# Gated stage: half centred beside its squares, root put into copies of the mixing weights, first mixing three steps later

## The chip, the cores and the metric

One core of a Trainium2 chip runs the whole program in one launch. The metric is the device time of that core in microseconds, the median of several executions. Data lie in float32 with the 128 partitions as rows of a tile of positions; a matrix product is made of three TensorE passes on a high and a low part.

## The reference

Sixteen stages over 256 positions of 1024 numbers, for two models one after the other: feed-forward stages, one mixer of each kind per layer, and an embedding stage. The change is in the second stage, the gated mixer (N = 2048 numbers per half, 8 groups of 256, blocks of 128 positions):

```python
z = jax.nn.gelu(h @ w_in + b_in)
u, v = jnp.split(z, 2, axis=-1)
mean = jnp.mean(vf, axis=-1, keepdims=True)
var = jnp.mean(jnp.square(vf - mean), axis=-1, keepdims=True)
v = (vf - mean) * lax.rsqrt(var + LN_EPS) * v_gain
ws = jnp.where(mask[None], w_s, 0)
s = jnp.einsum('gij,bcjgd->bcigd', ws, v) + b_s.T[None, None, :, :, None]
y = (u * s).reshape(B, S, GMLP_WIDTH)
return y @ w_out
```

The mean and the variance belong to a position j, and j is the index over which the mixing product sums. So the root of position j may stand with v (a row of it) or with column j of ws.

## The kernel before

The program is written out by hand for each engine; the order on an engine is the order of the code, and semaphores join the engines. There are two tiles t of 128 positions. `made`, `moved`, `product` and the like are counters: one semaphore each, raised by one engine in its program order, so that a wait for an entry is a wait for all before it.

Each matrix layer (`linear`, L505 to L507) goes through its weights in parts of two 128-row slices by 512 columns. The input layer of the gated stage has 8 blocks of 512 output columns, 4 parts each (part i, 32 in all), in the order v, v, v, v, u, u, u, u. A step is the three matmuls of one slice and one tile, so a part is 4 steps and block b has steps 16b + 1 to 16b + 16; part i has steps 4i + 1 to 4i + 4. `during(step)` puts other TensorE work ahead of a step.

For each part ScalarE makes the rounded copy `wh` (L623, "cast" below) and VectorE the remainder `wl` (L809, "remainder i"). There are seven buffers of each, so both work up to seven parts ahead: in the loop over parts, turn i handles part i + 7. Raw weights come from SyncE's queue in chunks of two parts, into three buffers; a chunk is asked for when the remainders of the chunk three before it are made.

The gated stage's own work:

- After block b, VectorE puts scale and bias on the two tiles' result (L1259, "bias work of block b"), and ScalarE's gelu writes v into `TMP` (blocks 0 to 3, L1209, with a sum) or u into `gU` (blocks 4 to 7, L1214).
- After block 3, `dve_layer_norm` (L1285 on): VectorE takes the mean (L1291, L1294), ScalarE sums the squares of v less the mean in four pieces, tile t and half a of 1024 columns, order (0,0), (0,1), (1,0), (1,1) (L1223). VectorE adds the halves (L1296), POOL makes the root (L1001, L1003), and VectorE centres and scales (L1303) and multiplies by v_gain (L1307), piece by piece, half 0 of both tiles first.
- v_gain and the bias rows are copied by DMA from POOL's queue to all partitions (`spread`, L996) into three buffers `bc`; a copy waits until its buffer's last reader is done. The second half of v_gain takes the buffer of the bias of blocks 2 and 3.
- `pe_gmlp_mix(c)` (L1173) multiplies two groups of v by the masked, turned mixing weights `gW`, for both tiles, into banks 6 and 7. The mixings c = 0, 1, 2 stand ahead of steps 82, 98 and 114, and c = 3 ahead of step 127.
- `dve_gmlp_gated(c)` (L1277) adds b_s and multiplies by u. `pe_gmlp_turn` (L1183) transposes the result in two turnings per mixing (ahead of steps 90 and 91 for c = 0), using banks 6 and 7 in turn, ScalarE copies it to `gYH` (L1233), VectorE makes its remainder `gYL` (L1283). Only then is the bank free for the next mixing.

On VectorE, turn i of the loop is: gating if i is 20, 24 or 28; turned remainder if i is 22, 26 or 30; the remainder of part i + 7; bias work if i is 3, 7, 11 and so on. In the text, "remainder 23" is that of part 23, made in turn 16.

## Time and profile before

| | |
|---|---|
| three timed runs | 2326.01, 2326.09, 2327.51 us; median 2326.09 |
| the profiled execution's own time | 2319.1 us |
| its span | 2317.3 us |
| mean granted TensorE clock | 0.988 |
| TensorE busy | 2245.4 us, 97% |
| VectorE, ScalarE, POOL busy | 63%, 50%, 8% |
| chain that ended last | TensorE 81%, VectorE 4%, ScalarE 2% |
| DMA | 395.60 MB, mean 171 GB/s |

The span is from the first to the last instruction of one execution taken by the profiler, and its own time is 1.8 us longer; the timed runs are others. Times inside the trace are microseconds from the span's start. In a timeline an entry is one instruction, or several of one kind that follow each other (x2, x4), and the bracket gives the idle time before it and what ended it. PE is TensorE, DVE is VectorE, ACT is ScalarE.

### The profile page before, as it was taken

To read this page: it belongs to the slowest core of one execution; us is meant where nothing else is said; L and a number is where in the kernel's file an instruction comes from. 1 tells how busy PE (TensorE), PEld (TensorE's weight loads), DVE (VectorE), ACT (ScalarE), POOL (GpSimd) and SP (SyncE) were. 2 spreads that over 40 slices of the span, in tenths; PEclk is the share of its full clock that TensorE was granted. 3 is DMA by queue.
4 is the path that set the end of the run, shared out by engine and by line. 5 is a ranking of instruction groups with operands and counts; after the bars stand their busy time and mean duration, and the time that the engine had idled before them with its cause. 6 is when DMAs were issued, how large, how long until landed. Compare 5 with 4: busy or idle time off the path is not lost.

```text
span 2317.3 us, 33592 instructions
## 1 busy us (share of the span) xinstructions
PE 2245.4 (97%) x13285; PEld 1822.6 (79%) x13285; DVE 1467.5 (63%) x2077; ACT 1156.8 (50%) x1670; POOL 181.4 (8%) x289
## 2 busy tenths in 40 slices
PE   8999999999999899989999999999999999979998
PEld 6888788888888658768887888877888888758887
DVE  6656657656765877576567656656656765647655
ACT  5445545445544464254455445455445544545444
POOL 1001001001000011320011001001001000051001
PEclk9999999999999999999999999999999999989999
DMA  7556556554655540065556555525554655506553
GB/s 250 185 194 205 180 181 195 182 189 165 211 188 191 198 140 11 4 196 190 182 183 199 185 195 197 175 82 177 182 183 172 209 183 198 176 20 201 189 177 109
DMA packets 290074, 395.60 MB, mean 171 GB/s; under 512 B 11736, under 2 KB 193312, under 8 KB 289920
## 3 DMA queue, kind: packets, MB, share of 16 engines
q1 hardware_dynamic: 285072, 377.20, 49.0%
q0 software_dynamic: 4704, 16.20, 2.0%
q8 instruction: 107, 1.75, 0.3%
q14 instruction: 47, 0.39, 0.1%
q10 hardware_dynamic: 144, 0.07, 0.0%
HBM read 392.37 MB, written 1.05 MB: 170 GB/s over the span
## 4 chain that ended last, share of the span: by engine, by line
PE 81%; DVE 4%; ACT 2%; issue 1%; POOL 1%; DVEq 0%; POOLq 0%; ACTq 0%
PE bank L505 24%; PE bank L507 24%; PE bank L506 24%; PE bank L531 1%; PE bank L519 1%; DVE qPS L1863 0%; PE bank L2507 0%; PE bank L2501 0%; PE bank L1435 0%; DVE wl L809 0%; ACT JUNK L630 0%; ACT qPS L1808 0%; PE bank L2518 0%; PE bank L1921 0%; POOL rSM L1003 0%
## 5 line engine op out<-in xcount | busy, mean ns | idle before, releaser
L809 DVE TENSOR_TENSOR wl<-raw,wh 128x1024 fp32r<-128x1024 f32 x708 | 858.8, 1223 | 566.5 <-ACT wh L623 566.2
L623 ACT ACTIVATE wh<-raw 128x1024 fp32r<-128x1024 f32 x708 | 744.3, 1058 | 654.8 <-PE bank L507 633.5
L505 PE MATMUL bank<-wh,XH 128*128 128x512 f32 x2000 | 804.5, 402 | 19.4 <-DVE XL L2132 4.7
L506 PE MATMUL bank<-wl,XH 128*128 128x512 f32 x2000 | 783.8, 392 | 0.0
L507 PE MATMUL bank<-wh,XL 128*128 128x512 f32 x2000 | 783.7, 392 | 0.0
L505 PEld LDWEIGHTS bank<-wh,XH 128*128 128x128 f32 x2000 | 378.4, 189 | 109.8 <-issue 24.9
L507 PEld LDWEIGHTS bank<-wh,XL 128*128 128x128 f32 x2000 | 377.9, 189 | 82.1
L506 PEld LDWEIGHTS bank<-wl,XH 128*128 128x128 f32 x2000 | 378.8, 189 | 73.1 <-issue 0.5
L505 PE MATMUL bank<-wh,AH 128*128 128x512 f32 x704 | 276.0, 392 | 0.0
L507 PE MATMUL bank<-wh,AL 128*128 128x512 f32 x704 | 274.1, 389 | 0.0
L506 PE MATMUL bank<-wl,AH 128*128 128x512 f32 x704 | 274.1, 389 | 0.0
L507 PEld LDWEIGHTS bank<-wh,AL 128*128 128x128 f32 x704 | 132.1, 188 | 27.8
L506 PEld LDWEIGHTS bank<-wl,AH 128*128 128x128 f32 x704 | 132.2, 188 | 26.7
L505 PEld LDWEIGHTS bank<-wh,AH 128*128 128x128 f32 x704 | 132.2, 188 | 26.6
L1024 POOL TENSOR_SCALAR ST<-ST 128x1 f32<-128x1 f32 x32 | 8.6, 268 | 1363.2 <-ACT JUNK L630 1363.0
L723 ACT ACTIVATE AH<-bank 128x512 fp32r<-128x512 f32 x88 | 52.8, 600 | 114.6 <-PE bank L531 114.6
L927 DVE TENSOR_TENSOR AL<-bank,AH 128x512 fp32r<-128x512 f32 x88 | 60.8, 691 | 58.1 <-ACT AH L723 58.1
L957 DVE SCALAR_TENSOR_TENSOR att<-att,ST,bank 128x256 f32<-128x256 f32 x176 | 84.6, 481 | 6.2
L753 ACT ACTIVATE att<-bank,ST 128x256 f32<-128x256 f32 x176 | 72.5, 462 | 12.7 <-POOL ST L1064 12.7
L954 DVE SCALAR_TENSOR_TENSOR att<-att,bank 128x256 f32<-128x256 f32 x176 | 72.9, 414 | 5.2 <-ACT att L753 5.2
L635 ACT ACTIVATE XH<-CT 128x512 fp32r<-128x512 f32 x60 | 37.2, 628 | 77.4 <-DVE CT L826 72.7
L630 ACT ACTIVATE JUNK<-bank 128x512 bf16<-128x512 f32 x48 | 28.4, 591 | 55.2 <-PE bank L507 55.0
(332 smaller groups left out, 1720.1 us busy)
## 6 DMA issues: line engine op xcount, KB each, us to landing
raw<-in_ffn_w_dram SPq DMA_DIRECT2D x182, 512.0 KB, 4.6
raw<-in_ffn_wi_dram SPq DMA_DIRECT2D x176, 512.0 KB, 4.6
raw<-in_ffn_w_dram SPq DMA_DIRECT2D x40, 1024.0 KB, 4.9
raw<-in_ffn_wo_dram SPq DMA_DIRECT2D x40, 1024.0 KB, 4.9
raw<-in_a_wqkv_dram SPq DMA_DIRECT2D x18, 1024.0 KB, 4.8
raw<-in_a_w_in_dram SPq DMA_DIRECT2D x16, 1024.0 KB, 5.6
raw<-in_b_w_in_dram SPq DMA_DIRECT2D x12, 1024.0 KB, 4.9
bc<-in_norm_g_dram POOLq DMA_DIRECT2D x16, 512.0 KB, 5.2
```

What stands on the lines that cost most here:

```text
L505: pe.e.matmul(o, a, h, start=(k == 0), stop=False)
L506: pe.e.matmul(o, a, l, start=False, stop=False)
L507: m = pe.e.matmul(o, b, h, start=False, stop=(k == layer.nk - 1))
L623: act.e.activation(self.wh[j % N_W][:, 0:p.size], self.raw[p.chunk % N_RAW][:, p.at:p.at + p.size], ACT.Copy).then_inc(*self.rounded.up(j))
L630: act.e.activation(self.JUNK[:, 0:x.shape[-1]], x, ACT.Square, accum_out=total).then_inc(*self.squared.up(*key))
L635: act.e.activation(self.XH[:, 4 * b:4 * b + 4, t * P:(t + 1) * P], self.CT[b][:, :, :], ACT.Copy).then_inc(*self.x_hi.up(n, t, b))
L723: act.e.activation(self.AH[:, 2 * b:2 * b + 2, :], bank.rearrange("p (k s) -> p k s", k=2), ACT.Copy).then_inc(*self.hid_hi.up(n, b))
L753: act.e.activation(self.att[b % 3][:, t * FB:(t + 1) * FB], self.pair((n, "up", b))[t][:, 0:FB], ACT.Tanh, scale=sc[:, t:t + 1]).then_inc( ...
L809: dve.e.tensor_tensor(self.wl[j % N_W][:, 0:p.size], self.raw[p.chunk % N_RAW][:, p.at:p.at + p.size], self.wh[j % N_W][:, 0:p.size].bitca ...
L927: dve.e.tensor_tensor(lo, bank.rearrange("p (k s) -> p k s", k=2), hi.bitcast(F32), ALU.subtract).then_inc(*self.hid_lo.up(n, b))
L954: dve.e.scalar_tensor_tensor(x, x, 1.0, pair[:, 0:FB], ALU.add, ALU.mult).then_inc(*self.gate.up(n, b, t))
L957: dve.e.scalar_tensor_tensor(x, x, sc[:, T + t:T + t + 1], pair[:, FB:2 * FB], ALU.mult, ALU.mult).then_inc(*self.gated.up(n, b, t))
```

## The change

It does five things in the gated stage.

1. VectorE's eight passes over v become four, (v + (-mean)) * v_gain in one instruction each, tile 0 first; each waits for the square sum of its own piece alone, as ScalarE reads v before it is overwritten. The addition of the variance's halves stands ahead of the last of them.
2. The root is multiplied into the mixing weights: `gW` becomes tile 0's (in place) and a new buffer `gWR[1]` tile 1's, two VectorE instructions of 128 x 1024. Position j is the partition of the turned weights, so the root is one number per partition. `gWR[1]` lies in the last quarter of `gYL`'s place.
3. The DMA of v_gain's second half is issued ahead of POOL's root instead of behind it.
4. On TensorE the first mixing goes from ahead of step 82 to ahead of step 85, its turnings from 90 and 91 to 92 and 93.
5. On VectorE the bias work of block 4 goes from turn 19 to turn 17, and the first gating from turn 20 to turn 19.

```diff
--- before.py
+++ after.py
@@ -316,6 +316,9 @@
         self.gYL = at("gYL", EO + 16384, [P, 16, S], F32R)
 
 
+        self.gWR = [self.gW, at("gWR", EO + 28672, [P, 8, P], F32)]
+
+
         wide = [P, T, D]
         self.R = at("rR", EO, wide, F32)
         self.K = at("rK", EO + 8192, wide, F32)
@@ -1145,10 +1148,11 @@
                                            self.ident[:, :])
                     m.then_inc(*self.turned.up("ws", q))
             for c in range(3):
-                if step == 16 * (5 + c) + 2:
+                if step == 16 * (5 + c) + (5, 2, 2)[c]:
                     self.pe_gmlp_mix(pe, c)
-                if step in (16 * (5 + c) + 10, 16 * (5 + c) + 11):
-                    self.pe_gmlp_turn(pe, 2 * c + step % 16 - 10)
+                turn = 16 * (5 + c) + (12, 10, 10)[c]
+                if step in (turn, turn + 1):
+                    self.pe_gmlp_turn(pe, 2 * c + step - turn)
             if step == 16 * 7 + 15:
                 self.pe_gmlp_mix(pe, 3)
 
@@ -1166,11 +1170,11 @@
         self.place["pair", ("mix", g2)] = 3
         for t in range(T):
             bank = self.take_bank(pe, 6 + t, (self.made, "y", g2, t))
-            pe.wait_ge(self.made, "ws")
             pe.wait_ge(self.made, "v", g2 // 2, t)
+            pe.wait_ge(self.made, "wr", t)
             for h in range(2):
                 g = 2 * g2 + h
-                m = pe.e.matmul(bank[:, h * 256:(h + 1) * 256], self.gW[:, g, :],
+                m = pe.e.matmul(bank[:, h * 256:(h + 1) * 256], self.gWR[t][:, g, :],
                                 self.TMP[:, t, g // 4, (g % 4) * 256:(g % 4) * 256 + 256], start=True, stop=True)
             m.then_inc(*self.product.up("mix", g2, t))
 
@@ -1242,13 +1246,13 @@
             if i == 5:
                 dve.wait_ge(self.moved, "ws", 1)
                 dve.e.memset(self.gW[64:128, :, 0:64], 0.0).then_inc(*self.made.up("ws"))
-            if i >= 20 and i % 4 == 0:
-                self.dve_gmlp_gated(dve, i // 4 - 5)
+            if i == 19 or i > 20 and i % 4 == 0:
+                self.dve_gmlp_gated(dve, (i + 1) // 4 - 5)
             if i >= 20 and i % 4 == 2:
                 self.dve_gmlp_turned(dve, i // 4 - 5)
             self.leave(dve, p.j + N_W)
-            if i % 4 == 3:
-                b = i // 4
+            if i == 17 or i != 19 and i % 4 == 3:
+                b = 4 if i == 17 else i // 4
                 bias = self.place["bc", ("bias", b // 2)]
                 for t in range(T):
                     dve.wait_ge(self.used[t], layer.end[b])
@@ -1292,19 +1296,22 @@
             *self.made.up("mean"))
         dve.wait_ge(self.made, "mean")
         dve.e.tensor_scalar(nmean, mean, -1.0 / 2048, None, ALU.mult).then_inc(*self.made.up("nmean"))
-        dve.wait_ge(self.squared, "var", 1, 1)
-        dve.e.tensor_tensor(r, var[:, 0:T], var[:, T:2 * T], ALU.add).then_inc(*self.made.up("var"))
+        dve.wait_ge(self.made, "nmean")
+        for t in range(T):
+            for a in range(2):
+                g = self.place["bc", ("v_gain", a)]
+                x = self.TMP[:, t, a, :]
+                dve.wait_ge(self.squared, "var", t, a)
+                if (t, a) == (1, 1):
+                    dve.e.tensor_tensor(r, var[:, 0:T], var[:, T:2 * T], ALU.add).then_inc(*self.made.up("var"))
+                dve.wait_ge(self.d_bc[g], "v_gain", a)
+                dve.e.scalar_tensor_tensor(x, x, nmean[:, t:t + 1], self.bct[g][:, :], ALU.add, ALU.mult).then_inc(
+                    *self.made.up("v", a, t))
         dve.wait_ge(self.rs, "ln")
-        dve.wait_ge(self.made, "nmean")
-        for a in range(2):
-            g = self.place["bc", ("v_gain", a)]
-            for t in range(T):
-                x = self.TMP[:, t, a, :]
-                dve.e.tensor_scalar(x, x, nmean[:, t:t + 1], r[:, t:t + 1], ALU.add, ALU.mult).then_inc(
-                    *self.made.up("centred", a, t))
-                dve.wait_ge(self.d_bc[g], "v_gain", a)
-                dve.wait_ge(self.made, "centred", a, t)
-                dve.e.tensor_tensor(x, x, self.bct[g][:, :], ALU.mult).then_inc(*self.made.up("v", a, t))
+        dve.wait_ge(self.made, "ws")
+        for t in (1, 0):
+            m = dve.e.tensor_scalar(self.gWR[t][:, :, :], self.gW[:, :, :], r[:, t:t + 1], None, ALU.mult)
+            m.then_inc(*self.made.up("wr", t))
 
     def pool_gmlp(self, pool, n):
         A = self.A
@@ -1319,12 +1326,10 @@
                 self.pool_rs(pool, n)
             if q == 3:
                 for a in range(2):
-                    if a == 1:
-                        r = self.cols(T, "lnr")
-                        pool.wait_ge(self.made, "var")
-                        self.rsqrt(pool, r, 1.0 / 2048, LN_EPS, "ln")
                     i = self.spread(pool, A["a_v_gain"][0, a * 1024:(a + 1) * 1024], "v_gain", a)
                     self.bc_busy[i] = [(self.made, "v", a, 1)]
+                pool.wait_ge(self.made, "var")
+                self.rsqrt(pool, self.cols(T, "lnr"), 1.0 / 2048, LN_EPS, "ln")
             c = order[q]
             i = self.spread(pool, bias[c * 512:c * 512 + 1024], "bias", q)
             self.bc_busy[i] = [busy[q]]
```

VectorE, the place from the mean of block 3's end to the last pass (ST holds the small columns, bc_76 and bc_77 the halves of v_gain). Before:

```order
L1291 TENSOR_REDUCE ST<-ST 128x2
L1294 TENSOR_SCALAR ST<-ST 128x2
L1296 TENSOR_TENSOR ST<-ST 128x2
L1303 TENSOR_SCALAR TMP<-TMP,ST 128x1024
L1307 TENSOR_TENSOR TMP<-TMP,bc_76 128x1024
L1303 TENSOR_SCALAR TMP<-TMP,ST 128x1024
L1307 TENSOR_TENSOR TMP<-TMP,bc_76 128x1024
L1303 TENSOR_SCALAR TMP<-TMP,ST 128x1024
L1307 TENSOR_TENSOR TMP<-TMP,bc_77 128x1024
L1303 TENSOR_SCALAR TMP<-TMP,ST 128x1024
L1307 TENSOR_TENSOR TMP<-TMP,bc_77 128x1024
```

Now:

```order
L1295 TENSOR_REDUCE ST<-ST 128x2
L1298 TENSOR_SCALAR ST<-ST 128x2
L1308 SCALAR_TENSOR_TENSOR TMP<-TMP,ST,bc_76 128x1024
L1308 SCALAR_TENSOR_TENSOR TMP<-TMP,ST,bc_77 128x1024
L1308 SCALAR_TENSOR_TENSOR TMP<-TMP,ST,bc_76 128x1024
L1306 TENSOR_TENSOR ST<-ST 128x2
L1308 SCALAR_TENSOR_TENSOR TMP<-TMP,ST,bc_77 128x1024
L1313 TENSOR_SCALAR gWR<-gW,ST 128x1024
L1313 TENSOR_SCALAR gW<-gW,ST 128x1024
```

Eight passes became four, the addition moved from ahead of all to ahead of the last, and two scalings of the weights follow.

VectorE, the place behind it, from remainder 23 on (wl is a part's remainder, att the output of the bias work, gU the gated half). Before:

```order
L809 TENSOR_TENSOR wl_69<-raw_54,wh_62 128x1024
L809 TENSOR_TENSOR wl_70<-raw_55,wh_63 128x1024
L809 TENSOR_TENSOR wl_64<-raw_55,wh_57 128x1024
L809 TENSOR_TENSOR wl_65<-raw_56,wh_58 128x1024
L1259 SCALAR_TENSOR_TENSOR att_80<-bank,ST,bc_75 128x512
L1259 SCALAR_TENSOR_TENSOR att_78<-bank,ST,bc_75 128x512
L1277 SCALAR_TENSOR_TENSOR gU<-bank,MT,gU 128x256 x4
L809 TENSOR_TENSOR wl_66<-raw_56,wh_59 128x1024
L809 TENSOR_TENSOR wl_67<-raw_54,wh_60 128x1024
L1283 TENSOR_TENSOR gYL<-bank,gYH 128x512 x2
```

Now:

```order
L812 TENSOR_TENSOR wl_69<-raw_54,wh_62 128x1024
L812 TENSOR_TENSOR wl_70<-raw_55,wh_63 128x1024
L1263 SCALAR_TENSOR_TENSOR att_80<-bank,ST,bc_75 128x512
L1263 SCALAR_TENSOR_TENSOR att_78<-bank,ST,bc_75 128x512
L812 TENSOR_TENSOR wl_64<-raw_55,wh_57 128x1024
L1281 SCALAR_TENSOR_TENSOR gU<-bank,MT,gU 128x256 x4
L812 TENSOR_TENSOR wl_65<-raw_56,wh_58 128x1024
L812 TENSOR_TENSOR wl_66<-raw_56,wh_59 128x1024
L812 TENSOR_TENSOR wl_67<-raw_54,wh_60 128x1024
L1287 TENSOR_TENSOR gYL<-bank,gYH 128x512 x2
```

The bias work of block 4 went ahead of two remainders, the gating ahead of one, and the turned remainder has three remainders ahead of it since the gating instead of two.

POOL, the place of the two halves of v_gain. Before:

```order
L996 DMA bc_76<-in_a_v_gain_dram 128x1024
L1001 TENSOR_SCALAR ST<-ST 128x2
L1003 TENSOR_TENSOR ST<-ST,NEG 128x2
L996 DMA bc_77<-in_a_v_gain_dram 128x1024
L996 DMA bc_75<-in_a_b_in_dram 128x1024
```

Now:

```order
L999 DMA bc_76<-in_a_v_gain_dram 128x1024
L999 DMA bc_77<-in_a_v_gain_dram 128x1024
L1004 TENSOR_SCALAR ST<-ST 128x2
L1006 TENSOR_TENSOR ST<-ST,NEG 128x2
L999 DMA bc_75<-in_a_b_in_dram 128x1024
```

The copy of the second half went ahead of the two instructions of the root.

## Rows read from the trace of the kernel before

**Rows 1.** The page: busy time, share of the span and instructions of each engine.
```profile
PE 2245.4 (97%) x13285; PEld 1822.6 (79%) x13285; DVE 1467.5 (63%) x2077; ACT 1156.8 (50%) x1670; POOL 181.4 (8%) x289
```

**Rows 2.** Windows: window, length, busy of PE, PEld, DVE, ACT, POOL, PEclk, DMA, GB/s.
```profile
260.00:270.00 10.00, 7.17 (x22) 5.17 (x21) 8.77 (x9) 3.42 (x4) 1.80 (x3) 0.71 0.16 52
270.00:280.00 10.00, 7.74 (x32) 6.18 (x31) 9.72 (x14) 4.34 (x6) 0.00 (x0) 0.84 0.64 223
```

**Rows 3.** Timeline of PE: start us, us, engine, line, operation [idle before, releaser].
```profile
260.36 0.39 PE L505 MATMUL bank<-wh,XH 128*128 128x512 f32 x1
...
263.24 1.10 PE L1173 MATMUL bank<-TMP,gW 128*128 128x256 f32 x4 [2.04 <-DVE TMP L1307]
265.13 2.07 PE L1173 MATMUL bank<-TMP,gW 128*128 128x256 f32 x4 [0.79 <-DVE TMP L1307]
...
271.67 0.39 PE L505 MATMUL bank<-wh,XH 128*128 128x512 f32 x1
...
276.83 0.66 PE L1183 MATMUL bank<-ident,gU 128*128 128x128 f32 x4 [2.26 <-DVE gU L1277]
...
284.86 1.89 PE L1173 MATMUL bank<-TMP,gW 128*128 128x256 f32 x8
...
287.28 0.39 PE L505 MATMUL bank<-wh,XH 128*128 128x512 f32 x1
...
292.05 0.60 PE L1183 MATMUL bank<-ident,gU 128*128 128x128 f32 x4
...
293.19 0.60 PE L1183 MATMUL bank<-ident,gU 128*128 128x128 f32 x4
```

**Rows 4.** Timeline of DVE (VectorE), same columns.
```profile
251.97 1.40 DVE L1259 SCALAR_TENSOR_TENSOR att<-bank,ST,bc 128x512 f32<-128x512 f32 x2
...
259.67 0.16 DVE L1296 TENSOR_TENSOR ST<-ST 128x2 f32<-128x2 f32 x1 [5.13 <-ACT JUNK L1223]
260.95 0.81 DVE L1303 TENSOR_SCALAR TMP<-TMP,ST 128x1024 f32<-128x1024 f32 x1 [1.12 <-POOL ST L1003]
...
269.03 4.62 DVE L809 TENSOR_TENSOR wl<-raw,wh 128x1024 fp32r<-128x1024 f32 x4
...
275.11 1.66 DVE L1277 SCALAR_TENSOR_TENSOR gU<-bank,MT,gU 128x256 f32<-128x256 f32 x4
```

**Rows 5.** Timeline of ACT (ScalarE): the first of four squares.
```profile
254.57 1.15 ACT L1223 ACTIVATE JUNK<-TMP,ST 128x1024 bf16<-128x1024 f32 x1 [0.43 <-DVE ST L1294]
```

**Rows 6.** Timeline of POOL (GpSimd).
```profile
233.50 0.53 POOL L996 DMA_DIRECT2D bc<-in_a_v_gain_dram  x1 [12.54 <-DVE att L1259]
259.92 0.19 POOL L1001 TENSOR_SCALAR ST<-ST 128x2 f32<-128x2 f32 x1 [25.89 <-DVE ST L1296]
260.20 0.72 POOL L1003 TENSOR_TENSOR ST<-ST,NEG 128x2 f32<-128x2 f32 x1
260.88 1.00 POOL L996 DMA_DIRECT2D bc<-in_a_v_gain_dram  x1
```

**Rows 7.** One line's durations; landing of the bc copies; DMA issues (KB, us to landing).
```profile
L2255 DVE SCALAR_TENSOR_TENSOR rK<-rTB,rK x2: 1225/1226/1226, 848.6 to 867.6; 128x1024 f32<-128x1024 f32 x2
...
DMA to landing us min/median/max: 4.2/4.7/7.0
...
raw<-in_a_w_in_dram SPq DMA_DIRECT2D x15, 1024.0 KB, 5.8
...
bc<-in_a_v_gain_dram POOLq DMA_DIRECT2D x1, 512.0 KB, 4.3
```

**Rows 8.** Timelines of DVE and of POOL in a later stage.
```profile
549.88 3.49 DVE L809 TENSOR_TENSOR wl<-raw,wh 128x1024 fp32r<-128x1024 f32 x3
...
551.24 1.04 POOL L1001 TENSOR_SCALAR ST<-ST 128x1 f32<-128x1 f32 x1
```

**Rows 9.** Longest wait of PE near 1575 us, and a window there.
```profile
PE bank L505 <- DVE XL L832: 1.8, 1, 1.8
...
1574.00:1576.00 2.00, 0.90 (x4) 0.37 (x2) 1.90 (x4) 0.95 (x3) 0.03 (x1) 1.00 0.87 265
```

## The prediction

> **What bounds the kernel now.** I read the page first: TensorE is busy 97% of the span [rows 1], so a change pays only where TensorE pauses or runs at its lower clock. A table of windows then shows where that is in the gated stage: 260 to 280 us, with TensorE busy for 7.17 and 7.74 us in 10 and a mean granted clock of 0.71 and 0.84 [rows 2]. TensorE's own order of time [rows 3] says what happens there, in four places. Before step 82 it waits for the normalised half: the first mixing starts at 263.24, though step 82 was due at 261.04 (step 81 starts at 260.36, and a step, three matmuls, takes 0.68 us: seven of them lie between 287.28 and 292.05), and the second half of it waits again. Then the clock is at 1.2 GHz until step 86 at 271.67. The first turning waits 2.26 us for the gated product. And the clock falls a second time.
>
> The loss, from step 81 at 260.36 to step 99 at 287.28 [rows 3]: 26.92 us. At 2.4 GHz the same work needs 18 steps x 0.68 = 12.24; two mixings at 1.74 each (the one at 284.86 and the step behind it take 2.42, less 0.68); two turnings at 0.46 (292.05 to 293.19 is 1.14 for one and a step). That is 16.64, so **10.28 us is all there is to win** in this place.
>
> What TensorE waits for is VectorE's queue [rows 4]. ScalarE sums the squares in four pieces from 254.57, one each 1.28 us (to the add at 259.67) [rows 4, 5]; VectorE does nothing in between. The root comes back from POOL 1.28 us after the add started (259.67 to 260.95) [rows 4, 6]. Only then do eight passes begin, 8.08 us to 269.03, then four remainders (4.62), the bias work of block 4, and the gating at 275.11, which ends at 276.77; the turning starts 0.06 later.
>
> **The edits, costed.** *Passes.* Gone: the eight that took 8.08 us of VectorE. Added: 4 fused passes and 2 scalings of the weights. The fused form of this size takes 1.226 us [rows 7], a queue of such operations advances by 1.13 a piece (4.62 for four, less the overlap) [rows 4], and the scaling has the form and size of the old centring, 0.81 (260.95) [rows 4], advancing by about 0.73. In sum 6.5 us, but the fused passes need no root and so start beside the squares. Ahead of the root nothing else was on VectorE, so they take nobody's place.
>
> *When they run.* The (0,0) pass can start at 254.57 + 1.28 = 255.85 and ends at 257.1. The second now is (tile 0, half 1), and needs the second half of v_gain. Its DMA now stands ahead of the root in POOL's queue and waits only for the bias work of block 3, which ends at 251.97 + 1.40 = 253.37 [rows 4]; with the 0.25 us that VectorE's signal takes to POOL (259.67 to 259.92) [rows 6] it is issued at 253.62. Nothing on POOL is behind it until the add at 260.2. Such copies landed 4.2 to 7.0 us after their issue; the one of this half took 4.3 [rows 7], which I take: 257.9. So the pass starts at 257.95, not 257.13, the next at 259.09 (its square ended at 258.4), the add at 260.23, the last pass at 260.31, ending at 261.54.
>
> One issue took 1.00 us at 260.88, beside VectorE's centring at 260.95, the other 0.53 at 233.50 [rows 4, 6]. In the new place the issue meets no long VectorE operation. The Trainium skill (SBUF — State Buffer, the "DVE blocks DMA" trap) says that a DMA from the POOL queue cannot write its descriptors while VectorE runs an operation in a two-port mode. By it the landing would come 0.47 us sooner than my 4.3, and the sum below would be 9.8 instead of 9.3; I stay with the landing that was measured, and count the other as part of the forecast.
>
> *The root.* Now it is worked out while a VectorE pass with two SBUF inputs runs. The trace has that case: with three such subtractions running from 549.88, a POOL operation that takes 0.19 us by itself (259.92) took 1.04 from 551.24, up to the end of the subtraction beside it [rows 6, 8]. So I let POOL's first operation end when the last pass does, 261.6, and the power, 0.72 us [rows 6], at 262.42. Without this hold it is 260.23 + 1.28 = 261.51. The row shows it for a subtraction, not for the fused form. The Trainium skill (SBUF — State Buffer, "Who interferes with whom") says that any VectorE instruction with two SBUF inputs contends with a GpSimd one that reads SBUF. By it the fused form holds POOL too and the gain is the 9.3 below; if it does not, 10.2 (rival a).
>
> *Weights.* Scalings at 262.45 and 263.18, the second (tile 0's) done at 263.99. The mixing waits for the last of both, as its counter is the one of VectorE's order: **264.02**.
>
> *TensorE.* The first mixing is now ahead of step 85, due at 260.36 + 4 x 0.68 = 263.08. It pauses 0.94 us, in place of 2.04 and 0.79. A pause of 1.8 us elsewhere in this program left the clock at 1.00 [rows 9], so I assume 2.4 GHz throughout. Step 86 then starts at 264.02 + 2.42 = 266.44, step 92 is due at 270.52, and there stands the first turning.
>
> *The gating.* VectorE: remainders of parts 23 and 24 at 263.91 and 265.04, bias work of block 4 at 266.17 (its matmuls are long done), remainder 25 at 267.49, gating at 268.62, ending 1.66 later at 270.28. ScalarE's gelu of block 4 lies beside remainder 25. The turning finds it ready 0.2 us before its time: 2.26 us of wait gone, with hardly any reserve. The remainders that were moved behind the bias work and the gating (25 and 26) are needed at steps 101 and 105, after 279.
>
> *The second mixing* needs both banks, so the remainder of the first turnings, which now stands behind remainders 26, 27 and 28. Part 28's chunk is asked for after remainder 23, 265.14, and lands in 5.8 [rows 7] at 270.9; its cast ends at 272.0, its remainder at 273.7, the two turned remainders at 274.9. The mixing is due at 270.52 + 2 x 1.14 + 4 x 0.68 = 275.52. No wait, 0.6 us in reserve. Step 99 then starts at 277.94 instead of 287.28: **9.34 us gained**. Behind that the queues are in the order they had, and the rest of the program is shifted, not changed. The copy of the weights costs no DMA and shares only the place of the last quarter of gYL, which is written after the fourth mixing.
>
> Sum against the profiled execution: 2319.1 - 9.3 = 2309.8 us (span 2317.3 to 2308.0). The median of the three runs, 2326.09, is 7.0 above the profiled one; the same difference applied to it gives **2316.8 us**.
>
> **Rivals.**
> (a) *POOL is not held.* The fused pass is another form than the subtraction in the row, and its scalar operand may alter how it reads. Root at 261.51, weights at 263.08, no pause at step 85: gain 10.2, 2315.9. Against it: [rows 8].
> (b) *The shorter pause still brings the clock down.* For it: after 2.04 and 0.79 of waiting the clock fell [rows 2, 3]. Against it: [rows 9]. The Trainium skill (TensorE: Matmul & The Clock Gate, Part 1) says that the gate looks in windows that run free of the program, so a pause may count in one place and not in another; by it the one pause of rows 9 settles nothing, and this rival's time is the one to fear. Price: from 265.13 to 271.67 went 6.54 us, where the rest of mixing and step 82 (2.42 - 1.10) and steps 83 to 85 (2.04) need 3.36. So 3.2 less, gain 6.1, 2320.0.
> (c) *The second half of v_gain lands late*, 7.0 instead of 4.3 as the slowest such copy did. A pause of 0.94 + 2.7 = 3.6 and the clock's 3.2: gain 3.4, 2322.7, which counts as no change here. Against it: the median of such copies, 4.7 [rows 7].
> (d) *Slower*: the same place decides it, since the whole of VectorE's queue now stands behind that pass: the remainders, without which TensorE stops at step 93. Gain is 9.3 - 3.2 - d for a landing d later than 4.3; above d = 6.1 it is a loss, above 10.8 one that can be measured. A landing of 16 us, d = 11.7, gives 2326.1 + 5.6 = 2331.7. Nothing among the copies shown (7.0 at most) comes near.
> (e) *It does not do what it says*: if the pause before step 82 were TensorE's other wait (a bank) rather than the pass. The releaser is named as VectorE in both rows [rows 3], so I give it nothing of its own.
>
> **How the numbers follow.** A measurement of this kernel tells about 0.2%, 4.65 us, from no change. Forecast 0.59, (a) 0.15, (b) 0.16, (c) 0.07, (d) 0.03. Faster: 0.59 + 0.15 + 0.16 = 0.90; same 0.07; slower 0.03. The range: the best is all 10.28 and the 1.5 us by which the three runs differ, 2314.3; the other end is (b) with the same 1.5, 2321.5. (c) and (d), one in ten, lie outside, as may a part of the noise.
>
> **What would show it.** In the profile of the changed kernel: four fused passes beside the squares, the second starting at 258 and not at 257.1 (landing); POOL's first root operation about 1 us long (hold); one pause of TensorE near 1 us before the first mixing, none before the first turning; PEclk 1.00 throughout 260 to 280. A clock of 0.5 after the first mixing means (b). A wait of over 0.3 us at the first turning or the second mixing would prove my reserves wrong. A gain under 5 us or any wait on remainders at steps 93 to 105 would make the prediction wrong as a whole.

## The result and the profile after

| | before | changed |
|---|---|---|
| median of 4 runs | 2326.05 us | 2313.8 us |
| range | 2325.88 to 2327.51 | 2311.01 to 2316.76 |
| profiled execution, span | 2319.1, 2317.3 us | 2311.8, 2309.9 us |
| ratio, 95% interval | | 0.9962 (0.9945 to 0.9979) |

The change is faster, by 8.8 us by the ratio, with an interval from 4.9 to 12.8. The ratio is not the quotient of the two medians, which lie 12.3 us apart; how it was formed is not on record. The median of these four lies 0.5 us under the low end of the forecast range; two later series of 12 and 10 executions (below) had medians of 2316.3 and 2317.3.

Windows of the changed kernel, answering to [rows 2]:

```profile
260.00:270.00 10.00, 9.38 (x44) 7.61 (x43) 9.11 (x14) 5.57 (x8) 0.93 (x2) 1.00 0.44 143
270.00:280.00 10.00, 10.00 (x48) 8.34 (x47) 9.43 (x13) 5.35 (x7) 1.14 (x2) 1.00 0.87 304
```

The clock is at 2.4 GHz throughout and TensorE is busy 9.38 and 10.00 of 10, against 7.17 and 7.74. TensorE's timeline (start, us, engine, line, operation), answering to [rows 3]:

```profile
259.11 0.39 PE L508 MATMUL bank<-wh,XH 128*128 128x512 f32 x1
...
262.61 1.10 PE L1177 MATMUL bank<-TMP,gW 128*128 128x256 f32 x4 [0.62 <-DVE gW L1313]
263.55 1.03 PE L1177 MATMUL bank<-TMP,gWR 128*128 128x256 f32 x4
...
269.19 0.60 PE L1187 MATMUL bank<-ident,gU 128*128 128x128 f32 x4
...
270.32 0.60 PE L1187 MATMUL bank<-ident,gU 128*128 128x128 f32 x4
...
274.19 1.02 PE L1177 MATMUL bank<-TMP,gW 128*128 128x256 f32 x4
...
276.61 0.39 PE L508 MATMUL bank<-wh,XH 128*128 128x512 f32 x1
```

259.11 is step 81, 276.61 is step 99: **17.50 us where 26.92 were**, 9.42 less. One pause of 0.62 is left before the first mixing, 262.61; the turnings at 269.19 and 270.32 and the second mixing at 274.19 are issued one behind another. VectorE and then POOL, answering to [rows 4] and [rows 6]:

```profile
254.65 1.28 DVE L1308 SCALAR_TENSOR_TENSOR TMP<-TMP,ST,bc 128x1024 f32<-128x1024 f32 x1 [1.37 <-ACT JUNK L1227]
256.41 2.48 DVE L1308 SCALAR_TENSOR_TENSOR TMP<-TMP,ST,bc 128x1024 f32<-128x1024 f32 x2 [0.48 <-DMA bc<-in_a_v_gain_dram]
258.81 0.15 DVE L1306 TENSOR_TENSOR ST<-ST 128x2 f32<-128x2 f32 x1
258.88 1.28 DVE L1308 SCALAR_TENSOR_TENSOR TMP<-TMP,ST,bc 128x1024 f32<-128x1024 f32 x1
261.05 0.76 DVE L1313 TENSOR_SCALAR gWR<-gW,ST 128x1024 f32<-128x1024 f32 x1 [0.89 <-POOL ST L1006]
261.71 0.75 DVE L1313 TENSOR_SCALAR gW<-gW,ST 128x1024 f32<-128x1024 f32 x1
...
267.10 1.65 DVE L1281 SCALAR_TENSOR_TENSOR gU<-bank,MT,gU 128x256 f32<-128x256 f32 x4
...
272.07 1.28 DVE L1287 TENSOR_TENSOR gYL<-bank,gYH 128x512 fp32r<-128x512 f32 x2
```
```profile
252.42 0.53 POOL L999 DMA_DIRECT2D bc<-in_a_v_gain_dram  x1 [19.71 <-DVE att L1263]
259.05 1.16 POOL L1004 TENSOR_SCALAR ST<-ST 128x2 f32<-128x2 f32 x1 [6.10 <-DVE ST L1306]
260.29 0.72 POOL L1006 TENSOR_TENSOR ST<-ST,NEG 128x2 f32<-128x2 f32 x1
```

The first pass starts at 254.65, as its square ends, and the second waits until 256.41 for its DMA. The addition is at 258.81, the last pass at 258.88. POOL's first root operation takes 1.16 us instead of 0.19, to 260.21, just behind the end of that pass at 260.16: the hold. Gating ends at 268.75, 0.44 before the turning.

**Where the rest of the difference is.** The spans differ by 7.4, not 9.4. I compared the start of each of the 708 weight remainders in the two traces. Up to step 81 the changed kernel is 1.3 us ahead, because before had a fall of the clock at 19 us; behind the place it is 10.7 ahead, and that stays so to 763 us. Then 2.7 are lost up to 1035 us, and 0.5 more to the end. Nothing in those stages was changed. The windows of the two stages in which TensorE waits most (windows with mean granted clock), of before, of the changed kernel, and of the changed kernel run again (e1):

```profile
740.00:1040.00 300.00, 275.68 (x3629) 213.45 (x3628) 211.13 (x358) 136.37 (x210) 52.42 (x58) 0.97 0.34 113
2000.00:2110.00 110.00, 91.67 (x468) 68.30 (x467) 63.87 (x185) 58.19 (x144) 33.52 (x43) 0.91 0.30 98
```
```profile
740.00:1040.00 300.00, 274.91 (x3619) 212.69 (x3619) 211.73 (x362) 136.68 (x211) 52.45 (x58) 0.96 0.33 113
2000.00:2110.00 110.00, 91.63 (x465) 68.36 (x464) 64.51 (x178) 56.98 (x139) 36.42 (x46) 0.91 0.30 98
```
```profile
740.00:1040.00 300.00, 274.09 (x3599) 211.27 (x3598) 209.67 (x359) 133.29 (x207) 52.39 (x58) 0.95 0.33 108
2000.00:2110.00 110.00, 90.83 (x460) 67.60 (x459) 62.32 (x178) 56.53 (x141) 33.44 (x43) 0.89 0.29 93
```

0.97, 0.96 and 0.95 of full speed over 300 us of nearly the same work, and 0.89 in place of 0.91 later. Both kernels pause there, and in which of those pauses the clock falls differs from one execution to the next. The 86 executions of before spread from 2317.1 to 2330.4.

The largest single item is one fall near 840 us. Here are 30 us from the same point of the work, in the profile of before and in that of before run again (e2), whose span is 7.6 us longer:

```profile
835.00:865.00 30.00, 29.39 (x104) 18.09 (x103) 22.58 (x26) 18.69 (x29) 6.89 (x4) 1.00 0.46 155
```
```profile
833.00:863.00 30.00, 27.42 (x83) 16.53 (x82) 19.06 (x22) 14.86 (x23) 6.89 (x4) 0.83 0.33 101
```

Over this stretch e2 loses 6.6 us on before, and 2.0 more between 2060 and 2080 us. The fall near 840 is in ten of the fourteen traces, but in neither of the two compared above. e1 and e11, the changed kernel run again, have it as e2 has. Measured against e2 they keep the gain to the end: counted from ahead of the place, 9.4 and 9.5 us behind it, and 9.1 in both at the last remainder.

### The profile page after: what moved, and what is told of

Read it like the earlier page. It is cut to its first block, busy times and chain, and to the rows that moved or that the text cites. A ratio compares the mean times of both kernels' runs of the same rounds, so it can differ in the third digit from the quotient of the medians.

```text
span 2309.9 us, 33589 instructions
## 1 busy us (share of the span) xinstructions
PE 2240.7 (97%) x13285; PEld 1819.9 (79%) x13285; DVE 1466.0 (63%) x2075; ACT 1156.9 (50%) x1670; POOL 182.2 (8%) x289
## 4 chain that ended last, share of the span: by engine, by line
PE 92%; DVE 4%; ACT 2%; issue 1%; POOL 1%; DMA 0%; DVEq 0%; POOLq 0%; SPq 0%; ACTq 0%
PE bank L508 28%; PE bank L510 27%; PE bank L509 27%; PE bank L534 2%; PE bank L522 1%; DVE qPS L1868 0%; PE bank L2512 0%; PE bank L1440 0%; PE bank L2506 0%; ACT wh L626 0%; ACT JUNK L633 0%; ACT qPS L1813 0%; PE bank L2523 0%; PE bank L1926 0%; POOL rSM L1006 0%
## 5 line engine op out<-in xcount | busy, mean ns | idle before, releaser
L508 PEld LDWEIGHTS bank<-wh,AH 128*128 128x128 f32 x704 | 132.2, 188 | 26.8
```

What stands on the lines that cost most here:

```text
L508: pe.e.matmul(o, a, h, start=(k == 0), stop=False)
```

## The experiments

"The place" is always the stretch from the start of step 81 to the start of step 99, read from the profiled execution of each kernel. At full clock and without a wait it is 16.64. A letter such as A or B is a theory of the expectation printed above it.

| kernel | place, us | pause before the mixing | wait at the turning | ratio (95%) |
|---|---|---|---|---|
| before; e2 before again | 26.92; 26.83 | 2.04 + 0.79; 2.05 + 0.79 | 2.26; 5.10 | e2 0.9996 (0.9984 to 1.0009) |
| changed; e1; e11 | 17.50; 17.42; 17.35 | 0.62; 0.5; 0.5 | none over 0.2 | 0.9965 (0.9952 to 0.9978); 0.9971 (0.9959 to 0.9983) |
| e3 last pass behind | 17.20 | none | 0.34 | 0.9970 (0.9957 to 0.9983) |
| e4; e12 bias in gap | 16.65; 16.65 | none | none | 0.9973 (0.9961 to 0.9984); 0.9961 (0.9947 to 0.9975) |
| e5 order alone | 24.76 | 0.80 | 4.39 | 0.9997 (0.9984 to 1.0009) |
| e6 passes alone | 21.23 | 2.67 | none | 0.9990 (0.9979 to 1.0002) |
| e7 old VectorE order | 18.36 | 0.43 | 0.80 | one run, 2319.6 us |
| e8 old steps | 21.27 | 2.70 | none | one run, 2318.8 us |
| e9 queue 6.8 later | 25.98 | 7.31 | none | one run, 2326.0 us |
| e10 v_gain early | 17.15 | 0.23 | none | one run, 2309.7 us |

**e1 and e11, the changed kernel again.** Edit: none.

> The changed kernel once more, for the total. Theory A (the gain is the 9.4 us that the place from step 81 to step 99 gives, the rest of the first result's 12 us is clock elsewhere): ratio 0.996, median some 9 us under before, single runs some us apart with the falls of the clock outside the place; the place itself 17.5 us again, pause before the first mixing 0.6. Theory B (the change also speeds up something outside the place): ratio 0.9948 or less again, and a stretch outside the place that is shorter in this trace as in the first.

> The changed kernel a third time, for the total: if the gain is the place's 9.4 us and the rest is clock elsewhere, the mean over all its runs lies 9.4 us under the mean of before (ratio 0.9960); if earlier finishing costs something back later, 8 or less (0.9965 or more). Place 17.4 to 17.5 us again.

The place is 17.42 and 17.35. In both traces the start of every remainder outside the place lies as in the other traces but for jumps beside a fall of the clock and a drift of at most half a microsecond. So B of e1 fell: nothing outside is shorter. The low median of the first four is within chance (their mean is 1.9 us under that of the 22 later ones, with a standard error of 1.6). Over all 26 executions the changed kernel's mean is 2315.5 us (standard error 0.6), that of the 86 of before 2323.5 (0.3): 8.1 less, within 1.4 at 95%. As a ratio that is 0.9965, the value that e11 names for a cost later on; the interval only just reaches the 9.4 of the place, so the total does not decide between the two.

The same gap shows in every version with more than one timed run. The mean time less the place of the trace is 2296.6 us for before, and 2298.0 for the changed kernel, 2298.2 for e3, 2299.2 for e4 with e12, 2298.4 for e5 and 2299.1 for e6, with standard errors of 0.3 for before and 0.6 to 1.2 for the others. What makes up these 1.4 to 2.6 us is taken up at the end of the part on the prediction.

**e2, before against itself.** Edit: none.

> The kernel before, unchanged, against itself. Theory A: ratio 1.000; its trace shows 26.9 us from step 81 to step 99 in any case, and windows at 1.2 GHz outside the gated stage that differ in number from those of the first trace, with some us of span. Theory B: the windows outside lie as in the first trace and the span is 2317.3 again.

A holds: ratio 1, place 26.83, span 2324.9. Its TensorE rows hold a surprise:

```profile
261.60 1.10 PE L1173 MATMUL bank<-TMP,gW 128*128 128x256 f32 x4 [2.05 <-DVE TMP L1307]
263.50 1.13 PE L1173 MATMUL bank<-TMP,gW 128*128 128x256 f32 x4 [0.79 <-DVE TMP L1307]
...
275.20 1.11 PE L1183 MATMUL bank<-ident,gU 128*128 128x128 f32 x4 [5.10 <-DVE gU L1277]
```

The pauses before the mixing are those of before, but here the clock did not fall behind them; the wait at the turning is 5.10 instead of 2.26, and the turning starts 16.49 us after step 81 (258.71) instead of 16.47. VectorE's queue set that moment in both. So in before the first fall of the clock cost nothing: it made TensorE's work longer, and the wait behind it shorter. The windows of e2 that lie as those of [rows 2] do against step 81 say the same: 1.00 and 0.85, where before had 0.71 and 0.84.

```profile
258.00:268.00 10.00, 7.16 (x31) 5.41 (x30) 8.57 (x10) 3.79 (x4) 1.88 (x3) 1.00 0.14 52
268.00:278.00 10.00, 4.90 (x20) 3.81 (x19) 9.86 (x13) 3.75 (x5) 0.00 (x0) 0.85 0.66 215
```

**e3, is POOL held by the pass?** The fourth pass goes behind the scalings; `centre` holds the old body of the loop.

```diff
-        for t in range(T):
-            for a in range(2):
...
-                if (t, a) == (1, 1):
-                    dve.e.tensor_tensor(r, var[:, 0:T], var[:, T:2 * T], ALU.add).then_inc(*self.made.up("var"))
...
+        def centre(t, a):
...
+        for t, a in ((0, 0), (0, 1), (1, 0)):
+            centre(t, a)
+        dve.wait_ge(self.squared, "var", 1, 1)
+        dve.e.tensor_tensor(r, var[:, 0:T], var[:, T:2 * T], ALU.add).then_inc(*self.made.up("var"))
...
             m.then_inc(*self.made.up("wr", t))
+        centre(1, 1)
```

> The fourth fused pass goes behind the two scalings, so that no VectorE operation with two SBUF inputs runs while POOL works out the root. Theory held (POOL is held by the pass): POOL's first root operation falls from 1.16 to 0.19 us, the root comes 1.28 us after the addition instead of 2.24, the first mixing is ready by step 85 and its pause of 0.62 is gone; the gating ends 0.3 later, so the first turning waits some 0.7, and the place takes about 17.4 us. Rival (POOL's operation is long for another reason, its first after a long idle): it stays near 1.1 us, the mixing is ready 0.2 later at best, the place takes 17.5 or more.

POOL and VectorE:

```profile
260.14 0.19 POOL L1004 TENSOR_SCALAR ST<-ST 128x2 f32<-128x2 f32 x1 [5.89 <-DVE ST L1312]
260.41 0.72 POOL L1006 TENSOR_TENSOR ST<-ST,NEG 128x2 f32<-128x2 f32 x1
```
```profile
259.89 0.15 DVE L1312 TENSOR_TENSOR ST<-ST 128x2 f32<-128x2 f32 x1
261.17 0.75 DVE L1316 TENSOR_SCALAR gWR<-gW,ST 128x1024 f32<-128x1024 f32 x1 [1.12 <-POOL ST L1006]
```

0.19 instead of 1.16, and the root 1.28 us after the addition instead of 2.24. The hold is the pass, and not POOL's long idling, which is the same. The pause is gone; the turning waits 0.34, less than the 0.7 expected, and the place is 17.20 (expected 17.4).

**e4 and e12, the gap filled.** As e3, and the bias work of block 4 (its code moved into a function) goes between the addition and the root, the gating one turn forward:

```diff
+        self.dve_gmlp_bias(dve, n, 4)
         dve.wait_ge(self.rs, "ln")
...
-            if i == 19 or i > 20 and i % 4 == 0:
-                self.dve_gmlp_gated(dve, (i + 1) // 4 - 5)
+            if i == 18 or i > 20 and i % 4 == 0:
+                self.dve_gmlp_gated(dve, (i + 2) // 4 - 5)
...
-            if i == 17 or i != 19 and i % 4 == 3:
+            if i != 19 and i % 4 == 3:
+                self.dve_gmlp_bias(dve, n, i // 4)
```

> As e3, and the bias work of block 4 (one SBUF input, one PSUM input) fills VectorE's wait for the root; the gating stands ahead of remainder 25. Theory held: POOL's root operations take 0.19 and 0.72 beside it, mixing and turning both find their input ready, no pause of TensorE in the place: 16.7 us from step 81 to step 99, 0.8 less than the change. In the total that is below what can be told: ratio 0.9955 to 0.996. Rival: bias work with a PSUM input holds POOL too (first operation over 0.5 us) and the mixing pauses 0.3 us or more.

> e4 a second time: place 16.65 us again. In the total the 0.8 us less than the change cannot be told from it (each mean is known to about 1 us); ratio 0.9955 to 0.9970. If it lies at 0.9973 or above again, removing the last pauses here costs something elsewhere.

```profile
258.42 0.15 DVE L1315 TENSOR_TENSOR ST<-ST 128x2 f32<-128x2 f32 x1
258.49 1.40 DVE L1271 SCALAR_TENSOR_TENSOR att<-bank,ST,bc 128x512 f32<-128x512 f32 x2
259.81 0.74 DVE L1320 TENSOR_SCALAR gWR<-gW,ST 128x1024 f32<-128x1024 f32 x1
```
```profile
258.66 0.19 POOL L1004 TENSOR_SCALAR ST<-ST 128x2 f32<-128x2 f32 x1 [5.99 <-DVE ST L1315]
258.94 0.72 POOL L1006 TENSOR_TENSOR ST<-ST,NEG 128x2 f32<-128x2 f32 x1
```

Bias work reads a PSUM bank and one SBUF tile, and POOL's operations beside it take 0.19 and 0.72, as alone. No pause is left: 16.65 twice, all of the 10.28 us that the prediction found in the place. The total cannot show the last 0.8: the mean of 20 executions is 2315.9 (0.7), of the changed kernel 2315.5 (0.6). The ratio of e4, 0.9973, missed its expectation; that of e12, 0.9961, met its own, so the cost elsewhere that e12 was to find did not show again. In the profile this version is the shortest of all in the place; in the time it is not told from the change.

**e5, the order alone.** The kernel before with the new steps and VectorE's new order, the eight passes kept:

```diff
-                if step == 16 * (5 + c) + 2:
+                if step == 16 * (5 + c) + (5, 2, 2)[c]:
...
+                turn = 16 * (5 + c) + (12, 10, 10)[c]
...
-            if i >= 20 and i % 4 == 0:
+            if i == 19 or i > 20 and i % 4 == 0:
...
-            if i % 4 == 3:
+            if i == 17 or i != 19 and i % 4 == 3:
```

> Only the order is changed (first mixing ahead of step 85, turnings ahead of 92 and 93, bias work of block 4 in turn 17, gating in turn 19); the eight passes and POOL's order are those of before. Theory A (VectorE's queue behind the root sets the first turning, so the order alone gives what it moves in that queue): the turning starts 15.1 us after step 81 instead of 16.5, step 99 follows 7.4 later with up to 1.7 of clock, so the place takes 22.5 to 24.3 us against 26.9. Theory B (the three steps ahead of the mixing are what counts): the pause before the mixing and the clock's fall are gone and the place takes 20 us or less.

```profile
263.67 1.13 PE L1174 MATMUL bank<-TMP,gW 128*128 128x256 f32 x4 [0.80 <-DVE TMP L1308]
...
274.00 1.12 PE L1184 MATMUL bank<-ident,gU 128*128 128x128 f32 x4 [4.39 <-DVE gU L1278]
```

A: the turning starts 15.12 us after step 81 (258.88), as expected, after a wait of 4.39. The place is 24.76, 0.5 over the range: from the turning to step 99 it took 9.64 us where 7.42 are due at full clock, so the clock cost 2.2 and not the 1.7 I had allowed for. The mean granted clock is 0.66 in the ten microseconds below, which means 6.8 of them at the lower level, some of them inside the wait. The order alone wins 2.2 in the place. The ratio, 0.9997, does not show it; its interval, down to 0.9984, allows it.

```profile
270.00:280.00 10.00, 6.00 (x21) 5.05 (x22) 9.74 (x13) 5.36 (x7) 0.00 (x0) 0.66 0.84 287
```

**e6, the passes alone.** The change with TensorE's old steps (the edit of e8) and VectorE's old order (the edit of e7).

> Only the fused passes, the scaled weights and the earlier copy of v_gain; mixing, turnings, bias work and gating stand where they stood before. Theory A: the mixing is ready 3.5 us after step 81 but due at 0.7, a pause of 2.8; gating ends at 11.0; the place takes 19.8 us at full clock, up to 22.7 if the pause brings the clock down for as long as in the trace of before. Theory B (the order gives most): over 24 us.

```profile
261.60 1.44 PE L1177 MATMUL bank<-TMP,gW 128*128 128x256 f32 x4 [2.67 <-DVE gW L1313]
262.84 1.91 PE L1177 MATMUL bank<-TMP,gWR 128*128 128x256 f32 x4
```

A: the mixing starts 3.51 us after step 81 (258.09). From its start to step 99 the place needs 15.96 at full clock (16.64 less one step); it took 17.72, so 1.8 us is clock. 21.23 in all, 5.7 us won in the place. In the total less of it shows: the ratio is 0.9990, and its interval, 0.9979 to 1.0002, leaves out the 0.9975 that 5.7 us would be.

e5 and e6 add up to 7.9 in the place and together win 9.4. The 1.5 between come from the clock. Before pays 1.7 behind its turning (10.45 us from 276.83 to step 99, where 8.78 are due), e5 pays 2.2, e6 pays 1.8, and the changed kernel nothing. With these prices taken off, the order alone gives 2.7, the passes alone 5.8 and both 7.8; only both together also save the 1.7 of before.

**e7, VectorE's old order in the change.**

```diff
-            if i == 19 or i > 20 and i % 4 == 0:
-                self.dve_gmlp_gated(dve, (i + 1) // 4 - 5)
+            if i >= 20 and i % 4 == 0:
+                self.dve_gmlp_gated(dve, i // 4 - 5)
...
-            if i == 17 or i != 19 and i % 4 == 3:
-                b = 4 if i == 17 else i // 4
+            if i % 4 == 3:
+                b = i // 4
```

> The change with VectorE's old order (bias work of block 4 in turn 19, gating in turn 20). Theory A (the move in the queue is worth what the gating comes later): pause before the mixing 0.6 as in the change, gating ends 11.0 us after step 81 instead of 9.6, the first turning waits about 1.0, the place takes 18.4 us instead of 17.5. Theory B (the turning has more reserve than I worked out): 17.5 again.

```profile
262.82 1.10 PE L1177 MATMUL bank<-TMP,gW 128*128 128x256 f32 x4 [0.43 <-DVE gW L1313]
...
270.39 0.66 PE L1187 MATMUL bank<-ident,gU 128*128 128x128 f32 x4 [0.80 <-DVE gU L1281]
```

A: 18.36, expected 18.4. The move in VectorE's queue is worth 0.9.

**e8, TensorE's old steps in the change.**

```diff
-                if step == 16 * (5 + c) + (5, 2, 2)[c]:
+                if step == 16 * (5 + c) + (2, 2, 2)[c]:
...
-                turn = 16 * (5 + c) + (12, 10, 10)[c]
+                turn = 16 * (5 + c) + (10, 10, 10)[c]
```

> The change with TensorE's old steps (mixing ahead of step 82, turnings ahead of 90 and 91). Theory A: pause of 2.8 us before the mixing, no wait at the turning, 19.5 us without a fall of the clock. Theory B (rival b of the prediction, a pause of this length brings the clock down and costs its full price): up to 22.7 us, with a granted clock of 0.5 behind the mixing.

```profile
264.09 2.04 PE L1177 MATMUL bank<-TMP,gW 128*128 128x256 f32 x4 [2.70 <-DVE gW L1313]
265.93 1.77 PE L1177 MATMUL bank<-TMP,gWR 128*128 128x256 f32 x4
```

Between the two: the pause is 2.70 and the clock does fall behind it (the four matmuls of a bank take 2.04 instead of 1.10, and the window below shows 0.83). But it costs 1.8, not 3.2: the mixing starts 3.54 after step 81 (260.55), with 15.96 that is 19.50, and the place is 21.27. The three steps are worth 3.8 us: 2.1 of pause (2.70 less 0.62) and the rest clock. Beside e6 (21.23) this also shows that VectorE's new order is worth nothing with the old steps.

```profile
260.00:270.00 10.00, 7.30 (x26) 5.65 (x25) 9.11 (x14) 5.07 (x7) 1.87 (x2) 0.83 0.34 108
```

**e9, the queue 6.8 us later.** Six products into unused space stand ahead of the scalings, behind a wait for the last pass:

```diff
+        dve.wait_ge(self.made, "v", 1, 1)
+        for i in range(6):
+            dve.e.tensor_tensor(self.SCR[:, i, :], self.TMP[:, 0, i % 2, :], self.TMP[:, 1, i % 2, :], ALU.mult)
```

> The change with six more VectorE products (128 x 1024, into unused space) between the root and the scalings: VectorE's queue is 6 x 1.13 = 6.8 us later from there on, as with a v_gain that lands so much later. Theory A (rival d's sum: everything behind it moves with the queue, the clock adds its own): place 17.5 + 6.8 + 3.2 = 27.5 us, above the 26.9 of before. Theory B (the clock's fall behind the mixing is swallowed in part by the wait at the turning, or costs 1.8 as in e8): 24.3 to 26.1 us, still below before.

```profile
270.34 2.04 PE L1178 MATMUL bank<-TMP,gW 128*128 128x256 f32 x4 [7.31 <-DVE gW L1317]
```

B: 25.98. The pause of 7.31 brings the clock down for the mixing (2.04 and 1.89). The price is about the same again: the mixing starts 10.19 after step 81 (260.15), and from there a place at full clock needs 13.92 (16.64 less four steps of 0.68), so 24.11, and 1.9 is clock. Even this stays 0.9 under before, so rival (d) would turn into a loss at a delay of about 7.7, an estimate from this row (6.8 + 0.9), and not at 6.1.

**e10, v_gain's second half early.** Its copy goes to space of its own, issued beside that of the mixing weights:

```diff
+        pool.e.dma_start(self.gG2[:, :], A["a_v_gain"][0, 1024:2048].partition_broadcast(P)).then_inc(
+            *self.d_one["vg2"].up(by=16))
...
-                g = self.place["bc", ("v_gain", a)]
+                g = self.place["bc", ("v_gain", 0)]
+                gain = (self.bct[g], self.gG2)[a]
```

> The change with the second half of v_gain copied at the stage's start into space of its own, so that no pass waits for a copy. Theory A (the wait of 0.48 us for it is passed on to the addition, the root and the mixing): the addition starts 0.4 us sooner, as it then waits for the last square, and the pause before the first mixing falls from 0.6 to 0.2; place 17.1. Theory B (the last square sets the addition already): pause and place unchanged, 0.6 and 17.5.

```profile
254.62 1.28 DVE L1313 SCALAR_TENSOR_TENSOR TMP<-TMP,ST,gG 128x1024 f32<-128x1024 f32 x1
...
257.17 0.16 DVE L1308 TENSOR_TENSOR ST<-ST 128x2 f32<-128x2 f32 x1
```
```profile
260.98 1.10 PE L1178 MATMUL bank<-TMP,gW 128*128 128x256 f32 x4 [0.23 <-ACT wh L627]
```

A: the second pass no longer waits for its copy. The addition lies 0.69 us ahead of step 81 (257.86) instead of 0.30 (258.81 and 259.11), and the pause is 0.23. The bracket names ScalarE's `wh`, but the second scaling ended at 260.83, 0.15 us ahead of the mixing, as in the changed kernel (262.46 and 262.61); the mixing still follows the scalings.

## Why the prediction was right

*The place.* Forecast 9.34 us less; measured 9.42, 9.50 (e1) and 9.57 (e11) less than the 26.92 of before, each 0.09 fewer against e2. Right, and for its reasons. 16.64 as the floor was right to 0.01 (e4).

*Landing.* The copy was issued at 252.42, 0.30 us behind the end of block 3's bias work at 252.12; my 0.25 was read from the start of an operation, not from its end. The issue took 0.53, not 1.00. By the count of [rows 7] the copy took 3.9 us and not 4.3, and 3.7 to 3.9 in the ten traces that have it in this place. The Trainium skill (SBUF — State Buffer, the "DVE blocks DMA" trap) says that a DMA from the POOL queue cannot write its descriptors while VectorE runs an operation in a two-port mode, and the estimate made by it was 3.83. The ten traces agree with that, and the row I kept to was 0.4 too long; no run here separates this cause from others.

*The pause.* The second pass started 2.70 us ahead of step 81, forecast 2.41. From there to the mixing it was 6.20, forecast 6.07. So the mixing came 3.50 behind step 81 instead of 3.66, and 0.78 behind the time at which it was due, instead of 0.94. The 0.62 in the bracket is the same pause, counted from the modelled end of the matmul before it, which lies 0.16 later.

*Hold.* Forecast: POOL's first operation ends with the pass. 1.16 us and 0.19 without (e3): right, and rival (a) fell. The Trainium skill (SBUF — State Buffer, "Who interferes with whom") says that a VectorE instruction with two SBUF inputs contends with a GpSimd one that reads SBUF, and that one with at most one SBUF input, outside the two-port modes, does not. The traces agree: 1.16 beside the pass, 0.19 beside the bias work with its one SBUF tile (e4).

*Passes.* 1.226 forecast, 1.28 measured in each of four, and two of them advance the queue by 2.40 instead of 2.28; scalings 0.81 forecast, 0.75 measured. They cancel in part: 0.13 more up to the mixing.

*Turning and second mixing.* Reserves of 0.2 and 0.6 forecast; measured 0.44 (268.75 to 269.19) and 0.84 (272.07 + 1.28 to 274.19). No wait, as forecast.

*Clock.* No fall after the pause in any of the changed kernel's three traces, as forecast. But **the price in rival (b) was mis-sized**: 3.2 against 1.8, 1.8 and 1.9 measured (e6, e8, e9). The windows of before, e6 and e9 show why:

```profile
264.00:272.00 8.00, 7.21 (x20) 5.48 (x19) 7.86 (x8) 0.00 (x0) 0.00 (x0) 0.57 0.10 27
```
```profile
261.00:267.00 6.00, 5.40 (x17) 4.39 (x18) 6.00 (x7) 0.47 (x2) 0.00 (x0) 0.72 0.53 165
```
```profile
270.00:280.00 10.00, 9.66 (x38) 7.88 (x39) 9.91 (x14) 3.88 (x5) 0.00 (x0) 0.80 0.69 212
```

The mean clock of 0.57 over 8 us means that before had 6.9 us at the lower level, about 6.0 of them behind 265.13, with TensorE at work. In e6 it was 3.4 us (0.72 over 6), in e9 some 3.6 behind the start of the mixing. The four matmuls of a bank take 2.07 us there and 1.10 at full clock, so what is lost is about half of such time: 3.0, 1.7 and 1.8. I had taken the longest of these falls as the price of any. And in before even that one cost nothing, since a wait for VectorE stood behind it (e2). With 1.8 rival (b) would have been at 2318.6. Rival (d) had the same term in it.

*The total.* **The step that failed is the last of the sum**: "The median of the three runs, 2326.09, is 7.0 above the profiled one; the same difference applied to it". There is no such offset. Both are draws from a spread of 13 us; between the two traces of before it was the clock outside the place that made the difference (8.6 us in two falls). Three runs within 1.5 us hid the spread, and the range allowed only these 1.5. The forecast 2316.8 is near the later medians by luck: its base, 2326.09, lies 2.6 above the mean of before, and the gain in the mean is 1.2 less than forecast. The first median is 3 us off it. Neither says anything about the mechanism; the place does.

What stays open: the mean over all executions fell by 8.1 within 1.4, the place by 9.4, and every version lies 1.4 to 2.6 us above before when its place is taken off (e11). That the place of before is 26.8 to 26.9 in every execution is known from two traces only. Both had the second fall of the clock, which cost 1.7 and 1.6 us; an execution without it would be shorter by that much. If most executions were without it, this would account for most of the gap in all the versions; no trace shows such an execution. The rival is that a program that finishes this stage earlier meets more falls later. Between e2 and the repetitions e1 and e11 only 0.3 us of the gain is lost later, between the first traces 3.2. Neither is settled.

## What to carry to other kernels

A factor that belongs to the contracted index can go into the other, smaller operand, and then nothing big waits for it: three of four fused passes ran beside the squares and the fourth beside the root, and two instructions on the weights were left behind the root. Look for what is at the head of the slow engine's queue at the moment the consumer waits, and shorten or reorder it before moving the consumer: in the place the order alone won 2.2 us, the passes alone 5.7, both 9.4. And judge a change of 0.4% by the stretch it touches, read from the trace, with the total over tens of executions only as a check.

## What the runs showed of the hardware

- The same program took 2317.1 to 2330.4 us in 86 executions. In the traces the difference lies where the granted clock fell to 1.2 GHz in stages with pauses of TensorE (0.95 to 0.97 in the mean over 300 us of nearly the same work); a single fall near 840 us made 6.6 us between two executions of the same kernel.
- A fall of the clock ahead of a wait for another engine cost nothing: the places of before and e2, with a mean granted clock of 0.71 and 1.00 in the stretch of the mixing, differ by 0.09.
- Pauses of 0.62 and less, and of 0.80 at a turning (e7), left the clock at 2.4 GHz. Behind 2.67 and 2.70 before a mixing it came down (e6, e8), as in that of 7.31 (e9). 2.04 and 0.79 in before had a fall behind them, 2.05 and 0.79 in e2 had none.
- A POOL operation on 128 x 2 numbers took 1.15 or 1.16 us beside a VectorE pass with two SBUF inputs, 0.19 beside one with a PSUM and an SBUF input, and 0.19 beside none.
- The copy of 512 KB from POOL's queue landed 4.3 us after an issue of 1.00 us beside VectorE's centring, and 3.7 to 3.9 us after issues of 0.53 us with no long VectorE operation beside them.
